# Scratch rows handed out one by one, and scans that overwrite their input, in a two-layer hybrid decoder on eight cores

## The reference, cut to what matters

```
x = layer_norm(ALPHA*x + 0.5*swiglu(x, ffn1));  x = layer_norm(ALPHA*x + mixer(x));  x = layer_norm(ALPHA*x + 0.5*swiglu(x, ffn2))

retention:  q, k = rotary(q), rotary(k)*DK**-0.5; o, s = chunkwise(q, k, v, s0); y = (silu(g) * groupnorm(o)) @ w_out
recurrence: gate_br, xb = split(x @ w_in);  gate_br = gelu(gate_br)
            xc = conv_b + sum(conv_w[j] * xp[:, j:j+T] for j in range(4))
            r, i = sigmoid(blockdiag(xc, w_a) + b_a), sigmoid(blockdiag(xc, w_i) + b_i)
            log_a = -8 * r * softplus(-lam);  a = exp(log_a);  u = sqrt(-expm1(2*log_a)) * (i * xc)
            h_t = a_t * h_(t-1) + u_t;        y = (gate_br * h) @ w_out
```

## Time and profile before

| | us |
|---|---|
| median of 3 runs | 3379.06 (3372.85 to 3383.19) |
| the profiled execution | 3402.35 |
| its span, slowest core (core 6) | 3400.8 |
| PE busy in the span | 3110.1 (91%) |
| DVE busy | 1450.9 (43%) |
| ACT busy | 1093.0 (32%), with 90 table loads, 115.5 |
| POOL busy | 705.5 (21%) |

### The profile page before, as it was taken

One profiled execution on the slowest core, in us unless ns is written; L12 is line 12 of the kernel. 1 busy time (PEld: TensorE's weight loads), 2 busy tenths in 40 slices (PEclk: granted clock), 3 DMA queues, 4 the chain that ended last, 5 costly groups with the idle time before them and its releaser, 6 DMA issues.

```text
span 3400.8 us, 54465 instructions; the slowest of 8 cores (3366.9 to 3400.8 us)
## 1 busy us (share of the span) xinstructions
PE 3110.1 (91%) x19104; PEld 1461.1 (43%) x19104; DVE 1450.9 (43%) x2637; ACT 1093.0 (32%) x1848; POOL 705.5 (21%) x916
## 2 busy tenths in 40 slices
PE   7999999899999976899899989998899999859996
PEld 3444344344444432344344444443344444324443
DVE  2117556631151197621321266555313313886113
ACT  2114433431131167311321144444212212663112
POOL 2022322210200234310210232222002002332011
PEclk9999999999999988899999999998999999879998
DMA  7532555434434323134544425554344343222441
GB/s 141 101 69 49 138 143 146 125 57 75 69 62 77 64 47 60 34 69 75 131 93 96 79 60 143 139 146 119 63 75 69 64 70 66 42 50 40 75 75 52
DMA packets 106955, 284.59 MB, mean 84 GB/s; under 512 B 16320, under 2 KB 16960, under 8 KB 106432
## 3 DMA queue, kind: packets, MB, share of 16 engines
q0 software_dynamic: 53280, 191.13, 33.3%
q1 hardware_dynamic: 53408, 89.98, 8.2%
HBM read 427.51 MB, written 44.65 MB: 139 GB/s over the span
## 4 chain that ended last, share of the span: by engine, by line
PE 83%; issue 5%; DVE 5%; ACT 4%; DMA 2%; POOL 0%; DVEq 0%; ACTq 0%; SPq 0%; POOLq 0%
PE ps L720 83%; DVE s_xa L755 2%; ACT s_fp L749 1%; DMA s_xa<-xT 1%; ACT s_xb L749 1%; PE ps L730 1%; ACT s_regA L749 1%; ACT s_regC L749 1%; ACT L749 1%; DMA s_regC<-sret 1%; DVE s_regB L760 0%; ACT s_regB L749 0%; DVE s_fp L1595 0%; DMA ret_s<-s_regC 0%; DVE s_regB L755 0%
## 5 line engine op out<-in xcount | busy, mean ns | idle before, releaser
L720 PE MATMUL ps<-s_xb,s_wb 128*128 128x512 bf16 (+1 forms) x10944 | 1757.9, 318 | 137.7 <-ACT s_xb L749 80.5
L720 PEld LDWEIGHTS ps<-s_xb,s_wb 128*128 128x128 bf16 x10944 | 820.3, 98 | 1055.6 <-issue 268.2
L156 POOL DMA_DIRECT2D s_wb<-wts x370 | 203.6, 551 | 1938.2 <-PE ps L720 1716.9
L749 ACT ACTIVATE s_sa<-ps 128x512 bf16<-128x512 f32 (+2 forms) x376 | 218.6, 582 | 1013.4 <-PE ps L720 1013.2
L720 PE MATMUL ps<-s_regB,s_wb 128*128 128x32 bf16 (+1 forms) x3856 | 500.7, 279 | 9.7 <-ACT s_fp L749 4.6
L720 PE MATMUL ps<-s_regA,s_wb 128*128 128x512 bf16 x1928 | 452.6, 383 | 45.0 <-DVE s_regA L755 38.8
L755 DVE TENSOR_TENSOR s_regB<-ps,s_sa 128x512 bf16<-128x512 f32 (+2 forms) x200 | 131.3, 657 | 555.6 <-PE ps L720 542.5
L720 PEld LDWEIGHTS ps<-s_regB,s_wb 128*128 128x128 bf16 x3856 | 249.9, 97 | 265.4 <-issue 30.1
L749 ACT ACTIVATE s_zq<-s_xa 128x512 bf16<-128x512 f32 x192 | 120.8, 629 | 594.0 <-DVE s_xa L760 479.9
L755 DVE TENSOR_TENSOR s_regA<-ps,s_sa 128x512 bf16<-128x512 f32 x176 | 121.7, 691 | 444.4 <-PE ps L720 430.6
L720 PEld LDWEIGHTS ps<-s_regA,s_wb 128*128 128x128 bf16 x1928 | 179.8, 98 | 250.2 <-issue 63.7
(11 more groups left out here) (115 smaller groups left out, 2067.3 us busy)
## 6 DMA issues: line engine op xcount, KB each, us to landing
s_wb<-wts POOLq DMA_DIRECT2D x354, 512.0 KB, 5.7
s_regC<-sret SPq DMA_DIRECT2D x128, 256.0 KB, 4.2
ret_s<-s_regC SPq DMA_DIRECT2D x128, 256.0 KB, 2.8
s_xa<-xT SPq DMA_DIRECT2D x32, 256.0 KB, 9.2
yT<-s_regA SPq DMA_DIRECT2D x16, 256.0 KB, 4.4
yT<-s_regB SPq DMA_DIRECT2D x16, 256.0 KB, 2.5
s_wb<-wts POOLq DMA_DIRECT2D x8, 416.0 KB, 5.1
s_regC<-rot SPq DMA_DIRECT2D x2, 1056.0 KB, 8.7
```

Source lines behind the costliest of these rows:

```text
L156: self.prog[eng].append(("o", lambda e, o=out, i=in_: e.dma_start(out=o, in_=i), d.h, 16))
L720: ins = e.matmul(out, l, r, start=(start and i == 0), stop=(stop and i == n - 1))
L749: return e.activation(out=out, in_=in_, func=func, **kw)
```

## The change

`FP` becomes 8 items of one row each. A new request, `Take(pool, n)`, asks for n items at once and is served only when n are free. `ln` and `rope` take two, `rec_gate` and `rec_scan` take one. `ln` now has two buffers (`Sb` for the sum, `fb` for the variance), and `rope` too. `rec_scan` writes the scan over its own input `u` (the tile `xc`), and gives its scratch row back right after the product with the square root instead of after the last product.

```
@@ Sched.run
+                    elif isinstance(r, Take):
+                        if len(r.pool.free) >= r.n:
+                            its = sorted(r.pool.free, key=lambda x: max(x[1].wt, x[1].rt))[:r.n]
+                            for it in its:
+                                r.pool.free.remove(it)
+                            self.advance(s, its)
...
-        FP = Pool("fp", [(fp_t[i], Buf(f"fp{i}")) for i in range(NFP)])
+        FP = Pool("fp", [(fp_t[i][:, j, :], Buf(f"fp{i}_{j}")) for i in range(NFP) for j in range(2)])
@@ ln (rope alike, with t1 and t2)
-            fp = yield FP
-            S, vv = fp[0][:, 0, 0:CN], fp[0][:, 1, 0:CN]
-            fb = fp[1]
+            f1, f2 = yield Take(FP, 2)
+            S, vv = f1[0][:, 0:CN], f2[0][:, 0:CN]
+            Sb, fb = f1[1], f2[1]
...
@@ rec_gate
-            ti, fb = fp[0][:, 0, 0:n], fp[1]
+            ti, fb = fp[0][:, 0:n], fp[1]
@@ rec_scan
-            sq, hs, fb = fp[0][:, 0, 0:n], fp[0][:, 1, 0:n], fp[1]
+            sq, fb = fp[0][:, 0:n], fp[1]
+            hs = u
             yield tt("pool", sq, a, a, MUL, (ab,), (fb,))
             yield act(sq, sq, AF.Sqrt, (fb, ctab_b), (fb,), bias=CT("quarter"), scale=-0.25)
             yield tt("dve", u, u, sq, MUL, (ub, fb), (ub,))
+            FP.put(fp)
...
-                     (ab, ub, hc_b[F]), (fb,), 0.1 + n * 0.0022)
+                     (ab, ub, hc_b[F]), (ub,), 0.1 + n * 0.0022)
...
-            yield tt("dve", gh, gh, hs, MUL, (fb, ghb), (ghb,))
-            FP.put(fp)
+            yield tt("dve", gh, gh, hs, MUL, (ub, ghb), (ghb,))
```

More of the change, by code:

```diff
@@ L215, in put, with __init__ @@
         self.free.append(it)
+class Take:
+    def __init__(self, pool, n):
+        self.pool, self.n = pool, n
+        self.name = pool.name
 class Op:
@@ L337, in run @@
                             self.advance(s, it)
+                            moved = True
+                            break
+                    elif isinstance(r, Take):
[4 more added lines that the diff above has]
+                            self.advance(s, its)
                             moved = True
@@ L978, in ln @@
                 if oc == 1:
[L979 removed]
+                    yield tt("pool", S, zs[0], zs[1], ADD, (zb[0], zb[1]), (Sb,))
                 elif 1 < oc < KC - 1:
[L981 removed]
+                    yield tt("pool", S, S, zs[oc], ADD, (Sb, zb[oc]), (Sb,))
             p = yield PS
[L983 removed]
+            yield mm(p[0][:, :], p[1], [(onesf_t[:], S), (onesf_t[:], zs[KC - 1])], (onesf_b, Sb, zb[KC - 1]))
             yield act(vv, p[0][:, :], AF.Square, (p[1],), (fb,))
@@ L1002, in apply @@
                 if final:
-                    yield tt("dve", y[0][:, kc, :], zs[kc], S, ADD, (zb[kc], fb), (y[1][kc],))
+                    yield tt("dve", y[0][:, kc, :], zs[kc], S, ADD, (zb[kc], Sb), (y[1][kc],))
                 else:
-                    yield tt("dve", zs[kc], zs[kc], S, ADD, (zb[kc], fb), (zb[kc],))
+                    yield tt("dve", zs[kc], zs[kc], S, ADD, (zb[kc], Sb), (zb[kc],))
                 left[0] -= 1
                 if left[0] == 0:
-                    FP.put(fp)
+                    FP.put(f1)
+                    FP.put(f2)
                 yield from ln_tail(th, kc, idx, final, g, y, exb, exa)
@@ L1189, in rope @@
                 p1b = p2b = its[0][1]
-            fp = yield FP
-            t1, t2, fb = fp[0][:, 0, 0:n], fp[0][:, 1, 0:n], fp[1]
+            f1, f2 = yield Take(FP, 2)
+            t1, t2 = f1[0][:, 0:n], f2[0][:, 0:n]
             for half, (ca, cb, op) in enumerate(((cos, sin, SUB), (sin, cos, ADD))):
-                yield tt("dve", t1, p1, ca, MUL, (p1b, rb), (fb,))
-                yield tt("dve", t2, p2, cb, MUL, (p2b, rb), (fb,))
+                yield tt("dve", t1, p1, ca, MUL, (p1b, rb), (f1[1],))
+                yield tt("dve", t2, p2, cb, MUL, (p2b, rb), (f2[1],))
                 if half == 1:
@@ L1197, in rope @@
                         PS.put(it)
-                yield tt("pool", dst[:, half, :], t1, t2, op, (fb,), (db[half] if isinstance(db, list) else db,))
-            FP.put(fp)
+                yield tt("pool", dst[:, half, :], t1, t2, op, (f1[1], f2[1]), (db[half] if isinstance(db, list) else db,))
+            FP.put(f1)
+            FP.put(f2)
             ev.on = True
@@ L1595, in rec_scan @@
             yield Op("dve", lambda e: e.tensor_tensor_scan(out=hs, data0=a, data1=u, initial=hc_t[:, F:F + 1], op0=MUL, op1=ADD),
-                     (ab, ub, hc_b[F]), (fb,), 0.1 + n * 0.0022)
-            yield cp("act", hc_t[:, F:F + 1], hs[:, CN - 1:CN], (fb,), (hc_b[F],)) if False else \
-                cp("pool", hc_t[:, F:F + 1], hs[:, CN - 1:CN], (fb,), (hc_b[F],))
+                     (ab, ub, hc_b[F]), (ub,), 0.1 + n * 0.0022)
+            yield cp("pool", hc_t[:, F:F + 1], hs[:, CN - 1:CN], (ub,), (hc_b[F],))
             lru_seq[F] = g * 2 + ci + 1
             if th.samp:
-                yield cp("pool", C["lro"][0][:, F, :], hs[:, CN:n].rearrange("p (b t) -> p b t", b=SG)[:, :, DEC_T - 1], (fb,),
+                yield cp("pool", C["lro"][0][:, F, :], hs[:, CN:n].rearrange("p (b t) -> p b t", b=SG)[:, :, DEC_T - 1], (ub,),
                          (C["lro"][1],))
             yield evg
-            yield tt("dve", gh, gh, hs, MUL, (fb, ghb), (ghb,))
-            FP.put(fp)
+            yield tt("dve", gh, gh, hs, MUL, (ub, ghb), (ghb,))
             evf.on = True
```

2 lines of the change are left out of this document (1 added, 1 removed).

## The result

| | before | after |
|---|---|---|
| median, us | 3378.43 (3372.85 to 3383.19, 4 runs) | 3427.71 (3424.99 to 3428.44, 4 runs) |
| ratio of the times | | 1.0145 (1.0127 to 1.0163) |
| the profiled execution | 3402.35 | 3427.46 |

The changed kernel is slower by 49 us. The forecast was slower by 22, at 3401, with a range up to 3426: the direction is right, the size is less than half of what came, and the time lies just outside the range.

The account below looks back on a forecast made before the run. PE bounds the kernel, with 83% of the chain and 291 us idle, partly from scratch shortage in the recurrences. Recurrences +20 and retention +2 make +22: 3379 + 22 = 3401, range 3364 to 3426.

Parts of the forecast that it names:

- +10 per group: Each group's recurrence, its three stretches summed: −11 + 39 − 18 = +10 us, so +20 for two groups.
- stretch 1: Recurrence, chunk 0's second projections to chunk 1's: the whole 10.9 us of idle gained, −11.
- stretch 2: Recurrence, chunk 1's second projections until its gates are done: PE waits behind ten scans, 75 us against 36.5, +39.
- stretch 3: Recurrence, chunk 1's gates done to chunk 0's next SwiGLU: 74 us, comparable figure 62 against 79.8, −18.
- Split buffers in the norm and the rope: Norm and rope: with earlier release, removes waits between operations of one engine; taken as 0, between −3 and +1.
- Together +2: Ends of both retentions: +6 in group 0, −4 in group 1, together +2 us, between −8 and +15.
- eight single rows: Recurrence: ten scans can be in flight and the starvation for scratch ends; with the block of scans, +10 us per group.
- earlier release: Taken with the split buffers as removing waits between operations of one engine: 0, between −3 and +1 in all.
- The clock after a long idle: PE's matmuls behind a long idle in stretches 2 and 3: slower, costing 2.8 us each, 5.6 per group.
- A: Rival: recurrence waits of 19.3 and 19.5 go and the scan block hides under PE's work; 3340 to 3367, chance 0.25.
- B: Rival: gains cancel the loss, chunk 1's stretch 2 growing by 29 instead of 39; within 10 us of 3379, chance 0.19.
- C: Rival: slower by retention, group 0's late units waiting 13.6 at each of two sites; 3413, chance 0.08 including a starvation rival.

Follow-up runs that it names:

- Experiments 1 and 8: 1: changed kernel, norm and rope each naming both rows in every dependence, ratio 1.0114 to before; 8: changed kernel, only the rope doing so, 1.0152.
- Experiment 4: Kernel before with its four pairs, scan over its own input, pair returned after the product with the square root; ratio 1.0137 to before.
- experiments 5 and 10: 5: changed kernel, norm and rope naming both rows, three tokens for chunk 0's first-half gates and scans, 0.9969; 10: plus two for chunk 1's first half, 0.9945.

## Why the prediction was wrong

The forecast fell short by 27 us. Of these 17 are the two recurrences' (+37 against +20), the term "+10 per group", and 10 are the retention's (+12 against +2). In both the instructions cost what I had read, and the order cost more than I had priced.

**Group 1's three stretches: right.** From the timeline of after, stretch 1 is 2997.00 - 2973.86 = 23.1 (the sum had 26.8), stretch 2 is 3071.63 - 2997.00 = 74.6 (75), stretch 3 is 3146.24 - 3071.63 = 74.6 (74). The wait of 36 on DVE's convolution copies, the second one ahead of the first SwiGLU matmuls (17.5 and 7.3 of small ones before it, where I had about 23 and 20), the block of ten scans, all came as written. Less the 12 us of SwiGLU matmuls done ahead, the three are 172.3 - 12 = 160.3, where before they were 154.0 (sum: 164).

**What the sum left out there.** +6.3 in the stretches is not the +16 that group 1's window shows. On cores 1 and 3 the three stretches grow by 5, and the window is longer at both ends, by 4 ahead of them and by 7 behind. Ahead, a wait of 4.69 on POOL's cast before chunk 1's first gates stands where one of 2.32 on ACT stood, and two groups of 72 small matmuls take 9.7 instead of 8.1 each. Behind, there is a new wait of 4.43 on ACT's `s_xb` after chunk 1's norm. I had cut the recurrence where the order differed most, and taken the places on either side as unmoved. So the term "+10 per group" was mis-sized: it measured +16 in group 1 and +21 in group 0.

**Group 0 is not group 1's copy.** I worked out one group and doubled it. The long waits of before and after are the same ones in both, but not the short ones: before (core 1), PE is idle 62.2 us in group 0's window and 69.5 in group 1's, the 7 spread over five places in waits that are 1 or 2 us longer in group 1. After (core 3) it is 85.9 and 87.6. Group 0 had fewer short waits for the new ones to swallow, so its net loss is 5 larger.

**The step that failed outright: the retention and the split buffers.** "Split buffers in the norm and the rope ... I take 0" and "Together +2": measured +12 in group 0 and nothing in group 1. I had argued from instruction times, and they are not the reason; the plan is. Experiments 1 and 8 show it: join the rope's rows, and the stage is back at 467 and 470. How the plan turns is read from the code and not shown by a run: with one buffer the planner takes the rope's second product to depend on the first, with two it doesn't, other choices follow, and group 0's sample units end up behind chunk 0's last norm. I had the moved units in the order and priced one wait for them, +6. Idle PE there grew by 8 (waits of 13.4, near the 13.6 of group 1 before, of 7.3 and small ones, where 13.4 and 5.6 stood), 4 came on top since the same matmuls ran at a lower granted clock, for which the sum had nothing, and the 4 that I took off for group 1 didn't come.

**Whose change it was.** I put the recurrence's part down to eight single rows, and "earlier release" stood in the term that I took as 0. Experiment 4 has four pairs and the same loss; the early return is enough to make ten scans ready at once. And the starvation that I called the fault to be cured had a second effect, which I had seen only from one side: it kept chunk 0's second half back until chunk 1's exps and scans were out of the way. With a hold at that one place (experiments 5 and 10) both waits go.

**The clock after a long idle.** I took 2.8 us for each. Behind the 36.19 the first 16 matmuls (8 of 512 and 8 of 32 columns) took 3.60, and the next such 16 took 2.08; behind the 17.46 the 16 of 512 took 4.98 against 16 x 0.21 = 3.4 at full clock: about 1.5 each, so this term was too high. PE's busy time over the whole span is the same in both kernels; the loss is idle time. The Trainium skill's rule on the default state (TensorE: Matmul & The Clock Gate, "What's actually happening") agrees in sign, with the windows' granted clock down from 0.92 to 0.90 and from 0.89 to 0.86.

**The rivals.** A (a gain, 0.25) and B (no change, 0.19) are out. C had the right places and the right sign, and at 3413 it still fell short: the retention cost its 12 and the recurrence more than the forecast at the same time. Its sum was also not what its words say: 3413 is one wait of 13.6 in the place of the +2, and one at each of two sites gives 3379 + 20 + 27 = 3426. My range stopped at 3426 because I let the upper bounds of two terms (+23 a group, +15 in the retention) hardly ever occur together; the recurrences took 37 of the 46 and the retention 12 of the 15.

## What to carry to other kernels

When a planner fixes the order, a buffer that is held shorter or split finer is a change of order, and its price is that order's, not that of the instructions it touches: compare the orders of every stage that uses the pool, also those where the edit looks like bookkeeping. A shortage can be what staggers two producers; before removing it, see which work will now be ready at once, and which PSUM bank or queue stands behind that block. And where one stage is summed up, carry the sum to the next places on both sides that didn't move, and do each group by itself.

## What the runs showed of the hardware

Ten scans with their products ran back to back on DVE in 27.1 us, and a scan took as long over its own input as into other memory (58.1 against 59.5 us for all 40). The first scan of the block took longer beside POOL's squares, as in the earlier trace rows:

```profile
3011.98 2.12 DVE L1615 TENSOR_TENSOR_SCAN s_regB<-s_regC,s_hc,s_regB 128x544 f32<-128x544 f32 x1
```

The Trainium skill (SBUF — State Buffer, "Who interferes with whom") says that a DVE instruction with two SBUF inputs contends with a GpSimd instruction that reads SBUF. The trace agrees: 2.12 us beside a square, 1.25 to 1.34 for the others of the block, for which POOL had only short copies to do.
